# Decoder layer on one Trainium2 core: experts' gate and up weights in one transfer with even columns first, two block borders gone, and the state-space operands set up a turn ahead

## What is computed

```python
def s5_branch(u, ...):                     # 32 groups of 16 channels, state of 64 complex numbers
    bu = einsum('blgc,gpc->blgp', ug, b_bar)
    _, states = associative_scan(combine, (a, bu), axis=1)
    y = real(einsum('blgp,gcp->blgc', states, c)) + d_skip * ug
def expert_block(acc, blk):                # e: expert, rows: its tokens, g: their gates
    yb = (silu(x2[rows] @ w_gate[e]) * (x2[rows] @ w_up[e])) @ w_down[e]
    return acc.at[rows].add(yb * g[:, None]), None
def reference(x, ...):
    x = layer_norm(ALPHA * x + token_mixer(x, ...), ln1_g, ln1_b)
    x = layer_norm(ALPHA * x + routed(x) + swiglu(x, shared), ln2_g, ln2_b)
```

## Time and profile before

| | us |
|---|---|
| median of three runs | 2113.94 |
| the profiled execution, own time | 2118.44 |
| its span, first to last instruction | 2116.7 |
| TensorE busy | 1997.8 (94%) |
| VectorE / ScalarE / GpSimd busy | 1132.1 / 771.5 / 540.9 |
| opening | 0 to 117.5 |
| attention and merge | 117.5 to about 1020 |
| projection, routing, shared expert | to 1227.7 |
| experts | 1227.7 to 2078 |
| second layer norm | to 2116.7 |

### The profile page before, as it was taken

How to read it: one execution, slowest core, us unless ns; L and a number is a source line. 1 busy time by engine, 2 the same in 40 slices (tenths; PEclk the granted TensorE clock), 3 DMA queues, 4 the chain that set the end, 5 groups by cost and what they waited for, 6 DMA issues and landing times. The chain is left out here.

```text
span 2116.7 us, 39190 instructions
## 1 busy us (share of the span) xinstructions
PE 1997.8 (94%) x12849; PEld 1735.7 (82%) x12849; DVE 1132.1 (53%) x3379; ACT 771.5 (36%) x1517; POOL 540.9 (26%) x969
## 2 busy tenths in 40 slices
PE   7889999999999889999899989999999999999992
PEld 7768889888988778888687778898888889999991
DVE  5833664456356652222556755555555556666654
ACT  4322453355144431111434023333333333333334
POOL 7145555200022300000100223334444332222120
PEclk9999999999999999999999999999999999999996
DMA  5522132211234521110341489999999999999995
GB/s 165 129 50 75 46 86 66 65 46 46 70 109 125 139 60 41 49 55 5 125 158 67 161 294 319 313 307 314 317 321 325 316 312 369 371 356 339 345 342 174
DMA packets 181200, 390.19 MB, mean 184 GB/s; under 512 B 26553, under 2 KB 121149, under 8 KB 155510
## 3 DMA queue, kind: packets, MB, share of 16 engines
q1 hardware_dynamic: 155568, 317.52, 41.7%
q0 software_dynamic: 25376, 71.46, 15.3%
q10 hardware_dynamic: 166, 0.05, 0.0%
HBM read 330.94 MB, written 64.98 MB: 187 GB/s over the span
## 5 line engine op out<-in xcount | busy, mean ns | idle before, releaser
L2600 PE MATMUL ps_gu<-xe,w_raw 128*128 128x144 f32 (+4 forms) x4224 | 536.3, 288 | 0.0
L2600 PEld LDWEIGHTS ps_gu<-xe,w_raw 128*128 128x128 f32 x4224 | 524.8, 197 | 0.2
L2642 ACT ACTIVATE w_hi<-w_raw 128x1024 fp32r<-128x1024 f32 x132 | 132.1, 1048 | 161.5 <-DMA w_raw<-in_exp_w_down 161.5
L2693 DVE TENSOR_TENSOR w_lo<-w_raw,w_hi 128x1024 fp32r<-128x1024 f32 x132 | 155.5, 1218 | 64.4 <-ACT w_hi L2642 64.3
L2556 POOL DMA_INDIRECT scr_acc<-y_main,out_idx x66 | 102.5, 1553 | 309.1 <-ACT y_main L2671 288.8
L1141 ACT ACTIVATE w_raw_first<-w_raw_first,o_stage 128x128 f32<-128x128 f32 (+1 forms) x192 | 86.4, 450 | 200.1 <-DVE o_stage L1089 199.2
L2671 ACT ACTIVATE y_main<-ps_ye,gate 128x512 f32<-128x512 f32 (+2 forms) x132 | 90.8, 688 | 123.5 <-PE ps_ye L92 123.5
L2647 ACT ACTIVATE xe<-ps_gu 128x512 f32<-128x512 f32 (+2 forms) x66 | 38.4, 581 | 216.2 <-PE ps_gu L2579 216.2
L2551 POOL DMA_INDIRECT scr_acc<-y_rest,out_idx x36 | 58.2, 1617 | 226.3 <-ACT y_rest L2668 226.3
L90 PE MATMUL ps_ye<-w_hi,e_h_hi 128*128 128x512 f32 (+2 forms) x264 | 109.9, 416 | 0.8 <-DVE e_h_lo L2720 0.7
L1808 DVE TENSOR_SCALAR e_sel<-e_slots,e_place 128x256 bf16<-128x256 bf16 (+1 forms) x536 | 104.6, 272 | 0.0
(11 more groups left out here) (460 smaller groups left out, 4774.3 us busy)
## 6 DMA issues: line engine op xcount, KB each, us to landing
w_raw<-in_exp_w_gate SPq DMA_DIRECT2D x66, 1024.0 KB, 8.2
w_raw<-in_exp_w_up SPq DMA_DIRECT2D x66, 1024.0 KB, 7.4
w_raw<-in_exp_w_down SPq DMA_DIRECT2D x66, 1024.0 KB, 8.1
w_raw_first<-in_w_in SPq DMA_DIRECT2D x24, 512.0 KB, 4.4
v_w_raw<-in_w_in SPq DMA_DIRECT2D x48, 256.0 KB, 2.7
merged<-in_x SPq DMA_DIRECT2D x14, 512.0 KB, 5.0
scr_att<-o_stage SPq DMA_DIRECT2D x16, 264.0 KB, 3.0
att_prev<-scr_att SPq DMA_DIRECT2D x16, 264.0 KB, 3.4
```

Of the source, the lines that this page charges most:

```text
L2600: ins = pe.matmul(ps_gu[:, 2 * w + c, 0:width], w3(raw[j][w])[:, k, c:2 * P:2], xT[:, k, 0:width], start=(k == 0), stop=(k == KD - 1))
L2642: act.activation(piece_of(hi[j], piece), piece_of(raw[j][DOWN], piece), ACT.Copy).then_inc(hi_made, 1)
L2693: tt(piece_of(lo[j], piece), piece_of(raw[j][DOWN], piece), piece_of(hi[j], piece).bitcast(F32), ALU.subtract).then_inc(lo_made, 1)
```

## The change

The host lays the experts' gate and up weights out anew: within each row of 256 the even columns come first, and for each expert and partition the 8 KB of gate are followed by the 8 KB of up. SyncE loads both with one 2 MB transfer, which waits until all 64 gate and up matmuls of item n-2 are done; TensorE waits once for both; a weight load reads 128 adjacent columns. The blocks of `mixer_input` and `project_and_route` are gone: they return one function for each engine, which `attention` and `experts` call first in their own blocks; their semaphores live to the end of the kernel. In the S5 loop TensorE transposes the operands of turn it+1 before it multiplies those of turn it (two sets of PSUM for the transposes), GpSimd makes `u_stage`, ScalarE writes the transposed inputs straight to `ut_all` and keeps the states.

```diff
     def load(n, j, width):
-        free = [sp.snap(v) for v in (4 * (n - 2) + 2, 4 * (n - 2) + 4, 2 * (n - 2) + 2)]
+        free = [sp.snap(v) for v in (4 * (n - 2) + 4, 2 * (n - 2) + 2)]
-        for w in (GATE, UP, DOWN) if width > P else (DOWN, GATE, UP):
+        for w in (0, 1) if width > P else (1, 0):
+            if w == 0:
+                sp.wait_ge(gu_done, free[0])
+                sp.dma_start(it.gate_up[j].unsqueeze(1), src[0][:, bass.ds(e, 1), :]).then_inc(ld[j][0], 16)
+            else:
                 if width > P:
                     sp.wait_ge(rest_done, rest_free)
+                sp.wait_ge(lo_made, free[1])
+                sp.dma_start(raw[j][DOWN].unsqueeze(1), src[1][:, bass.ds(e, 1), :]).then_inc(ld[j][1], 16)
...
+        pe.wait_ge(ld[j][0], 16 * (pair + 1))
         for w in (GATE, UP):
-            pe.wait_ge(ld[j][w], 16 * (pair + 1))
             for c in range(2):
                 for k in range(KD):
-                    ins = pe.matmul(ps_gu[:, 2 * w + c, 0:width], w3(raw[j][w])[:, k, c:2 * P:2], xT[:, k, 0:width],
+                    ins = pe.matmul(ps_gu[:, 2 * w + c, 0:width], w3(raw[j][w])[:, k, P * c:P * c + P], xT[:, k, 0:width],
...
+    laid = dict(inputs)
+    by_row = [np.asarray(laid.pop(name)).reshape(NE, D, P, 2).swapaxes(2, 3).reshape(NE, P, KD * 2 * P) for name in ("exp_w_gate", "exp_w_up")]
+    laid["exp_w_gate_up"] = np.stack(by_row, axis=2).reshape(NE, P, 2 * KD * 2 * P)
```

The border into the experts, and that into attention:

```diff
     @block.tensor
     def _(pe):
+        routing_tensor(pe)
...
+        pe.wait_ge(it.shares, NT - 1)
+        pe.wait_ge(it.idx_made, 2)
         turn_rows(0, 1, CAP)
+        pe.wait_ge(it.shares, NT)
...
     @block.tensor
     def _(pe):
+        opening_tensor(pe)
         for step in range(16):
+            if step == 4:
+                pe.wait_ge(first.states_kept, SSM_G // 4)
             pe_project(pe, step, 0)
```

The S5 loop, on TensorE, ScalarE and GpSimd:

```diff
-                for it in range(TURNS):
+            def turn_stage(it):
                     pe.wait_ge(staged, it + 1)
                     pe.wait_ge(ordered, it + 1)
+                if it >= 2:
+                    pe.wait_ge(copied_w, it - 1)
...
+            turn_stage(0)
+            for it in range(TURNS):
+                if it + 1 < TURNS:
+                    turn_stage(it + 1)
...
+            def responses(it):
                     act.wait_ge(turned, it + 1)
-                    act.activation(ut_stage[:, :, :], ps_ut, ACT.Copy).then_inc(copied_u, 1)
-                    act.activation(wt_stage[:, :, :, :], ps_wt, ACT.Copy).then_inc(copied_w, 1)
+                act.activation(ut_of(it), ps_ut[it % 2], ACT.Copy).then_inc(copied_u, 1)
+                if it:
+                    keep_states(it - 1)
+                act.activation(wt_stage[:, :, :, :], ps_wt[it % 2], ACT.Copy).then_inc(copied_w, 1)
                     act.wait_ge(k_done, it + 1)
...
+            for it in range(TURNS):
+                if it == 0:
+                    pool.wait_ge(u_evac, NT)
+                else:
+                    pool.wait_ge(turned, it)
+                pool.tensor_copy(u_stage[:, :, :].rearrange("p g (s c) -> p g s c", s=T),
+                                 u_tok[:, :, 64 * it:64 * it + 64].rearrange("p s (g c) -> p g s c", g=4)).then_inc(ordered, 1)
```

More of the change, by code:

```diff
@@ new lines, in opening_pool @@
+        def opening_pool(pool):
+            cst["write"](pool)
+            pool.memset(zeros[:, :], 0.0).then_inc(zero_ready, 1)
+            pool.wait_ge(lam_copied, 4)
+            t = {"raw": lam_raw, "scratch": scratch, "bits": bits, "rden": rden,
+                 "den_ready": den_ready, "rden_ready": rden_ready,
+                 "fac_ready": fac_ready, "pow_ready": pow_ready, "wide": [scratch_w[:, n, :] for n in range(4)]}
+            s5_parameters(pool, pool_ch, t, par)
+            pool.sem_inc(par_ready, 1)
+            for it in range(TURNS):
[5 more added lines that the diff above has]
+                                 u_tok[:, :, 64 * it:64 * it + 64].rearrange("p s (g c) -> p g s c", g=4)).then_inc(ordered, 1)
+            pool.wait_ge(ordered, TURNS)
+            pool.wait_ge(k_done, TURNS)
+            pool.wait_ge(v_copied, TURNS)
+            pool.wait_ge(stored, 16 * 5)
@@ L731, in at, with attention @@
             return t.sb(name, shape, dt)
-def attention(nc, m, cst, io, xT_hi, xT_lo, keep, scr, first, late, merged):
+def attention(nc, m, cst, io, xT_hi, xT_lo, keep, scr, first, late, merged, opening):
     with ExitStack() as stack:
         a = Memory(nc, stack)
+        opening_sync, opening_tensor, opening_scalar, opening_vector, opening_pool = opening
         RAW, WR = 3, 2
@@ L1739, in __init__ @@
             self.act = [early.sb("act_" + n, [P, KD, L], F32R) for n in ("hi", "lo")]
-        self.raw = [[m.sb(f"w_raw_{j}{w}", [P, 2048])[:, :] for w in range(3)] for j in range(2)]
+        self.raw, self.gate_up = [], []
+        for j in range(2):
+            both, down = m.sb(f"w_raw_{j}_gate_up", [P, 4096]), m.sb(f"w_raw_{j}_down", [P, 2048])
+            self.gate_up.append(both[:, :])
+            self.raw.append([both[:, 0:2048], both[:, 2048:4096], down[:, :]])
         self.x_main = [m.sb(f"x_main_{j}", [P, D])[:, :] for j in range(2)]
@@ L1751, in __init__ @@
         self.idx_f = m.sb("e_idx_f", [P, 2, 2])
-        self.ld = [[m.sem(f"ld_e{j}{w}") for w in range(3)] for j in range(2)]
+        self.ld = [[m.sem(f"ld_e{j}{w}") for w in ("gate_up", "down")] for j in range(2)]
         self.gathered = [m.sem("gathered_0"), m.sem("gathered_1")]
@@ L2435, in load_weights @@
+        return routing_sync, routing_tensor, routing_scalar, routing_vector, routing_pool
 def load_weights(sp, io, it, n, j, which):
     e = sp.value_load(it.item_e[0:1, bass.ds(n, 1)], min_val=0, max_val=NE - 1)
-    src = [io["exp_w_gate"][0].rearrange("e (q k) n -> q e (k n)", k=KD), io["exp_w_up"][0].rearrange("e (q k) n -> q e (k n)", k=KD)]
-    for w in range(2):
-        if w in which:
-            sp.dma_start(it.raw[j][w].unsqueeze(1), src[w][:, bass.ds(e, 1), :]).then_inc(it.ld[j][w], 16)
@@ L2442, in load_weights @@
-    if 2 in which:
-        sp.dma_start(it.raw[j][2].unsqueeze(1), io["exp_w_down"][0].rearrange("e (p c) n -> p e (c n)", c=2)[:, bass.ds(e, 1), :]).then_inc(it.ld[j][2], 16)
-def experts(nc, m, cst, io, scr, it, ln2, merged, out):
+    if 0 in which:
+        sp.dma_start(it.gate_up[j].unsqueeze(1), io["exp_w_gate_up"].rearrange("e q n -> q e n")[:, bass.ds(e, 1), :]).then_inc(it.ld[j][0], 16)
+    if 1 in which:
+        sp.dma_start(it.raw[j][2].unsqueeze(1), io["exp_w_down"][0].rearrange("e (p c) n -> p e (c n)", c=2)[:, bass.ds(e, 1), :]).then_inc(it.ld[j][1], 16)
@@ L2453, in experts @@
+def experts(nc, m, cst, io, scr, it, ln2, merged, out, routing):
     with ExitStack() as stack:
@@ L2857, in hybrid_layer @@
                     first = FirstWeights(o, io)
-                    mixer_input(nc, o, cst, io, xT_hi, xT_lo, keep, scr, first)
-                    attention(nc, o, cst, io, xT_hi, xT_lo, keep, scr, first, late, merged)
+                    parts = mixer_input(nc, o, cst, io, xT_hi, xT_lo, keep, scr, first)
+                    attention(nc, o, cst, io, xT_hi, xT_lo, keep, scr, first, late, merged, parts)
         it = ItemRows(m, merged, scr)
-        project_and_route(nc, m, cst, io, merged, it, scr)
+        parts = project_and_route(nc, m, cst, io, merged, it, scr)
         ln2 = {"gain": m.sb("ln2_gain", [P, D]), "shift": m.sb("ln2_shift", [P, D]), "loaded": m.sem("ln2_loaded")}
-        experts(nc, m, cst, io, scr, it, ln2, merged, out)
+        experts(nc, m, cst, io, scr, it, ln2, merged, out, parts)
 def kernel(**inputs):
```

1473 lines of the change are left out of this document (723 added, 750 removed).

## The result

| | before | changed |
|---|---|---|
| median of 4 runs, us | 2113.5 | 2143.1 |
| range, us | 2110.0 to 2120.8 | 2138.7 to 2147.3 |
| profiled execution, own time / span, us | 2118.4 / 2116.7 | 2140.0 / 2138.2 |

The ratio is 1.0123 (95% interval 1.0101 to 1.0146): the change makes the kernel slower, by 26 us by the ratio and 30 by the two medians, where the forecast was 2 us faster and the range ended at 2137. The prediction was wrong in sign and in size. Rival (c), a gap without weights, had 2142.

A forecast was written before the change was run, and what follows sets the result against it. The prediction took TensorE and the DMA engines as both full in the experts, meeting at the down weights. Borders -4 and -4, weight loads -3 and the 2 MB transfer +9 gave -2 us: 2112 for the median, range 2091 to 2137.

The forecast's parts named there:

- (c): Rival at items above 128 tokens: gathers and scatter cannot fill the gap, 1 us stall an item; 2142 us, chance 0.17.
- The 2 MB transfer: Experts' gate and up load: one transfer waiting for all matmuls costs +9 us, between -6 and +68.
- The halving: In the 2 MB term: a stall also delays the next need, so (0.9 - 0.43)/2 = 0.24 us an item.
- rival (b): Rival on weight transfers: fewer, larger ones are cheaper, stalls and the +9 us go; 2089 us, chance 0.13.
- Lower end: Of the 2 MB term, -6 us: 16 KB rows win more of the shared engines, 5.6 us of stalls go.
- upper bound of 68 us: Of the 2 MB term: the whole 3.9 us without weights arrives at the down weights above 128 tokens.
- Weight loads: Gate and up matmuls up to 128 tokens: step one saves 11.5 us, a quarter kept; -3 us, between 0 and -12.
- Borders and opening: Borders into attention (projection starts at 114.4, full clock) and into the experts: -4 us each, -8 together.
- The experts' border: Border into the experts: item 0's rest product 4.1 us earlier, then bound by item 1's down weights; -4 us.
- (a): Rival at items up to 128 tokens: TensorE keeps the 11.5 us weight-load gain; 2103.5 us, chance 0.17.
- (d): Rival at the opening: GpSimd's copy delays VectorE's setup, the experts' border gives 1 us only; 2121 us, chance 0.06.
- What would show it: Signs in the trace: ScalarE's wait for down at 160 tokens, stalls of some 14 us, DMA share below 0.96.

The follow-up runs named there:

- e1: Changed kernel with two 1 MB transfers instead of one, gate's after 32 of 64 matmuls as before, up's after all 64; 2107.7 us, ratio 0.9951.
- e13: The kernel of e1 run once more, as the base for others on one chip; ratio 0.9943.
- e3: Kernel before with one number changed: gate's transfer waits for all 64 matmuls, as up's does; 2135.6 us, ratio 1.0075.
- e2: Changed kernel with two 1 MB transfers instead of one, both issued after all 64 matmuls; 2134.1 us, ratio 1.0072.
- e7: Changed kernel with two 1 MB transfers, gate's issued after 48 of the 64 matmuls, some 2 us late; ratio 0.9981.
- e6: Changed kernel, still one late 2 MB transfer, but gate's and up's halves laid 1 MB apart, giving 8 KB rows; 2132.0 us, ratio 1.0065.
- e4: Kernel before with gate and up weights laid out even columns first and weight loads of step one; 2111.4 us, ratio 0.9969.
- e10: The kernel of e1 with the border of blocks ahead of attention put back, turn ahead kept; ratio 0.9965.
- e9: The kernel of e1 with the border of blocks ahead of the experts put back and nothing else; ratio 0.9983.

## Why the prediction was wrong

**What bounds the kernel** was read rightly: two full resources and the down weights as the point where they meet. That reading also held the answer, since at a share of 0.99 there was nothing to fill a gap with. It was not carried into the sum.

**The 2 MB transfer, +9 us forecast, is the step that failed.** Between e1 and the changed kernel lie 0.9947 (mean of e1 and e13) and 1.0128 (mean of its two ratios), 1.8% or 38 us. Two of the term's steps were wrong.

First, "Gathers and a scatter fill the gap: a scatter alone keeps the engines 0.89 busy, so 0.11 x 3.9 = 0.43 us of engine time is lost". The windows of the changed kernel from the landing of down at 1308.81 on, with the issue at 1311.43 (same columns as the earlier trace rows), then two windows of the kernel before at the same distance from the start of its item as the last two:

```profile
1308.80:1311.30 2.50, 2.46 (x19) 2.22 (x17) 1.40 (x2) 2.39 (x4) 0.00 (x0) 1.00 0.97 270
1311.30:1312.40 1.10, 1.07 (x10) 1.07 (x10) 1.10 (x2) 0.38 (x1) 0.00 (x0) 1.00 0.49 186
1312.40:1314.70 2.30, 1.53 (x20) 0.79 (x18) 2.10 (x9) 0.68 (x3) 0.00 (x0) 1.00 0.97 256
...
1314.10:1315.20 1.10, 1.10 (x14) 0.93 (x16) 1.00 (x6) 0.60 (x1) 0.00 (x0) 1.00 1.05 439
1315.20:1317.50 2.30, 2.30 (x22) 1.50 (x22) 0.80 (x4) 0.86 (x2) 0.00 (x0) 1.00 1.04 362
```

For 2.5 us gathers and a scatter do fill the gap, at a share of 0.97, as forecast. Then they run out, and from 1311.30 to 1312.40 half of the engines' time is idle, until the first packets of the new transfer start, 1.0 us after its issue. These start slowly. The queue that carries the weights (packets, MB, share of 16 engines), in the 0.3 us that begin at 1312.4 and in the microsecond that begins at 1314.7:

```profile
q1 hardware_dynamic: 12, 0.20, 390.8%
...
q1 hardware_dynamic: 24, 0.39, 110.2%
```

A view counts a packet with its whole time in the window in which it starts, or no share could be 390.8%. So the first 12 packets took 3.91 x 16 x 0.3 / 12 = 1.56 us each, and later ones 1.10 x 16 / 24 = 0.73: in 2.3 us the engines look full and move 256 GB/s, where the kernel before moves 362. By these rows, an estimate, the item loses 0.51 x 1.1 = 0.56 us to idle engines and 12 x (1.56 - 0.73) / 16 = 0.6 us to slow first packets, 1.2 us and not 0.43.

I had counted the gap from the landing of down to the issue of up, and gathers and a scatter that last as long as the gap. What had to be counted is from the last byte of down to the time at which the next transfer runs at full rate, less what the gathers and the scatter still have to move. Also the share of 0.89 in the earlier trace rows stood beside 113 GB/s: a scatter alone fills the share and moves little, while in the kernel before weights flow beside it.

Then "about the same for 24 items of 144": 0.24 us was more than enough for 160 tokens, where the late issue costs 0.08 to 0.12 us an item (e3 against before, e2 against e1). In the kernel before the 160 class has a share of 0.95 at 14.38 us, so 0.7 us of engine time an item was free. At 144 tokens, at 0.99, it costs 0.68 and 0.96, 16 and 23 us for the class. It has two parts there. In the items at full clock it is 0.40 us in both (14.13 against 13.73, 14.19 against 13.76), 10 us for the class. The rest, 7 and 13 us, are two and three items in which the waits of TensorE were followed by half clock. The prediction had no term for that. The halving rested on slack between two bounds that take turns; at a share of 0.99 there is one bound. The three times of issue in e1, e7 and e2 give 13.76, 13.98 and 14.19 us for the items at full clock: it begins at once and grows evenly, about 0.2 us for each 2 us. The ratios (0.9951, 0.9981, 1.0072) grow less evenly, and the items at half clock, which differ in number between executions, are a likely reason.

The Trainium skill ("DMA: Bandwidth & Descriptors", section on the anatomy of one DMA) gives a transfer about 2 us of fixed cost, most of it behind the last byte, and gives it for transfers issued by GpSimd. The rows above are of SyncE's queue and show what stands ahead of the bytes, 1.0 us; what stands behind the last byte no run here splits off. The estimate of 132 us in rival (b) applied the page's figure to SyncE's queue.

Second, "Lower end: rows of 16 KB win more of the shared engines". The sign was wrong. Beside e6, long rows cost 0.7%, 14 us. No rival had this. The upper bound of 68 us did hold both, and the range was too narrow because I put that bound outside it.

**Weight loads, -3 us.** Measured -6.6 in e4, within the bounds of 0 and -12. The mechanism and the 113 ns were right. Where the gain would be lost was half right: the 112 class keeps its 11.4 us, as forecast, while the 128 class keeps all of its gain, 11.51 to 11.17 (in one later execution with the same weight loads, that of e10, it did not: 11.57). The share of 1.02 or 1.03 at 128 tokens had made me count it as full; it moved 372 GB/s in e4 at a share of 1.03. The sign of a bound was the time to landing, 8.2 us at 128 tokens and 14.4 at 112, not the share. The rule of cachelines in the Trainium skill ("SBUF — State Buffer", section "Door 1: The DMA port swizzle"), by which a step of two in float32 costs nothing, does not hold for these weight loads: 119 ns against 113. By it e4 would have gained nothing.

**Borders and opening, -8 us.** e4 and e1, on one chip, differ by these alone: 0.9969 and 0.9951, 4 us. In detail: the projection starts at 112.7 (112.5 to 114.5 in the other executions with this opening) instead of the forecast 114.4, with its matmuls at 0.39 us at once, so at full clock (granted 1.00, 2.4 GHz); the gap before the last `ps_v` stayed 1.3 us and did not grow. The start at 117.52 in the earlier trace rows was a late one: e3 and e4, with the opening of before, start at 115.6 and 116.1. The turn ahead took 1.8 us, the same figure as forecast, but by luck, for the reason is another: neither a cut of the first turns nor GpSimd's copy, but the products of turn 7 that now stand behind the last transposes. The experts' border brought 2.2 us (e9) and not 4.1. What is late next there was named rightly, the down weights of item 1. Their place was not: they were issued at 1222.75, 3 us earlier than before (TensorE was 4 us earlier at 1164 us already), and landed at 1234.10 after 11.4 us, where it was 9.4 before.

**Rivals.** (a), the gain of the weight loads kept, is true of 128 tokens alone. (b) fell: e2 and e6, two transfers and one at the same time with the same rows, are equal within their intervals, so a transfer has no price of its own above some 6 us for the 66 of them. The Trainium skill's rule to batch transfers to 1 MB and more ("DMA: Bandwidth & Descriptors", section on bandwidth) gives no gain at 2 MB here, and at 144 tokens four transfers of 512 KB were the fastest. (d) fell as a whole. (c) had the number, 2142, and the mechanism for one half: its stall of 1 us in each item above 128 tokens came out as 0.75 and 0.77. But at 160 tokens that was not the gap, it was the row length, and at 144 part of it was the clock; that the number fits so well is partly luck. I gave it 0.17.

**What would show it** did: ScalarE's wait in the 160 class was announced as 5.2 us by the forecast and over 6.5 by (c), and was 6.03 and 6.71 in the items shown, 6.0 in the mean of the class. In e2 and e3, with the late issue and short rows, the means are 5.2 and 4.8: of the late issue alone the 5.2 was right. Stalls at the rest product were to be 14 us and were 13.1 at 144 tokens alone, with 10.1 us at the turning of the rows, which I had not named. The share fell to 0.95 at 144 tokens, below 0.96, the mark of (c); at 160 it was 0.95 before the change, so that mark told nothing there.

Open is why a row of 16 KB slows what shares the engines, beyond the slow start of the transfer; and which of the longer waits of TensorE bring the half clock and which don't. That the late issue costs 16 us in the kernel before (e3) and 26 in the changed one (e2 against e1) is, by the traces, mostly the number of items at half clock, two against three; the intervals nearly meet.

## What to carry to other kernels

Where two resources are both full, don't price a later transfer by the slack of the consumer. Take the time from the last byte of the transfer in flight until the next one runs at full rate, its slow start included, and subtract only work that exists and lasts that long. What is left counts in each turn in which the engines' share is near 1. Where it makes the bounding engine wait, look at that engine's granted clock behind the waits too. A free buffer should be refilled in pieces as soon as each piece is free: one wait made later by half a buffer cost 1.2%, and waits made earlier by a quarter won back the stalls of the tightest class, though shorter rows seemed to cost time where the engines were the bound.

## What the runs showed of the hardware

- One 2 MB transfer with a 16 KB row for each partition was 0.7% of the kernel slower than the same transfer with pieces of 8 KB (2147.0 and 2132.0 us), and the transfer behind it landed 11.5 instead of 10.7 us after the issue (medians at 160 tokens).
- With idle engines the first packets of a 2 MB load on SyncE's queue start 1.0 us after the issue, and the first twelve take 1.56 us each, against 0.73 for later ones (changed kernel, 1312.4 and 1314.7 us). Because a packet counts whole where it starts, a short window right behind a slow one reads too low.
- TensorE's granted clock fell to half for 3.4 or 6.8 us inside the experts' stage in each of the seven executions with a late gate transfer, in e2 behind 2.56 us of idle time, and in none of the eleven others; an item of 144 tokens with such a stretch took 17.0 to 19.5 us and not some 14.
- The mean share of the engines passes 1: 1.01 to 1.03, at 322 GB/s with gathers and scatters of 144 tokens and 374 with those of 128. At 0.99 before there was still room for 2% (13.73 to 13.46 us).
- Weight loads of 128 float32 columns beside matmuls of 128 columns: 113 ns from start to start with adjacent columns, 119 with a step of two.
- The same stretch of 885 us without any edit took between 883.8 and 888.8 us in all eighteen executions; differences under some 4 us were read from rows of the trace and not from a median.
